# One step list per engine, one weight chunk and one token tile per step, in a two-block transformer on one core

## The reference

```python
h = rms_norm(x, g1); proj = h @ w_in                       # 5128 columns
qa,ka,va,qb,kb,vb,f,gate = split(proj)                      # 8 + 8 heads of 64
o_a = causal softmax attention(rope(norm(qa)), rope(norm(ka)), va)
o_b = the same with norm(qb), norm(kb), vb and a decay from cumsum(log_sigmoid(f))
merged = sigmoid(gate0)*(o_a @ w_branch_moba) + sigmoid(gate1)*(o_b @ w_branch_fox)
x = x + merged @ w_out
u,g = split(rms_norm(x, g2) @ w_ffn_up); x = x + (silu(conv3(g))*u) @ w_ffn_down
# second block
hq,hf,hi,hg,sq,sk,sv,iq,ik,iw,mq = split(rms_norm(x, g3) @ w_in_2)   # 3656 columns
mixed = concat(hgrn(hq,hf,hi,hg), attention over the best 64 keys by an index score(sq..iw),
               attention over mem with rms_norm(mem) @ w_mem_kv)
x = x + mixed @ w_out_2
a,b = split(rms_norm(x, g4) @ w_ffn_in_2); x = x + (silu(a)*b) @ w_ffn_out_2
```

## Time and profile before

| | us |
|---|---|
| median of 3 runs | 795.67 (795.42 to 797.9) |
| the profiled execution | 799.01 |
| its span, first to last instruction | 796.9 |
| mean granted TensorE clock | 0.970 of full speed |
| PE busy | 752.3 (94%) |
| DVE busy | 525.8 (66%) |
| ACT busy | 472.6 (59%) |
| chain that ended last: PE, DVE, ACT | 78%, 11%, 7% |
| weights and inputs read | 127 MB, 161 GB/s over the span |

### The profile page before, as it was taken

The page is one execution under the profiler, slowest core; times in us unless marked ns, Lnnn a source line. Parts: engine busy times, 40 slices in busy tenths (PEclk is TensorE's granted clock), DMA queues, the critical chain, the costliest instruction groups (busy, mean ns, idle before and its releaser), DMA issues.

```text
span 796.9 us, 10804 instructions
## 1 busy us (share of the span) xinstructions
PE 752.3 (94%) x3887; PEld 623.8 (78%) x3887; DVE 525.8 (66%) x811; ACT 472.6 (59%) x746; POOL 11.9 (1%) x18
## 2 busy tenths in 40 slices
PE   7999989999979999999999889897689999999998
PEld 4887879987778888888888777675568888888886
DVE  3777776686566878767365457998845666766540
ACT  3765667784256788776163695655724765676430
POOL 0014000000000000000000000000000000000000
PEclk7999999999989999999999999998899999999999
DMA  8657464444156664454475435331033666655640
GB/s 276 238 162 242 151 183 148 150 158 158 53 185 212 211 210 160 157 185 159 158 234 162 139 110 178 106 107 66 15 107 106 215 207 211 211 183 183 224 123 26
DMA packets 70985, 128.86 MB, mean 162 GB/s; under 512 B 5575, under 2 KB 17823, under 8 KB 70944
## 3 DMA queue, kind: packets, MB, share of 16 engines
q1 hardware_dynamic: 70366, 125.91, 48.6%
q10 hardware_dynamic: 578, 2.40, 0.9%
HBM read 127.24 MB, written 1.05 MB: 161 GB/s over the span
## 4 chain that ended last, share of the span: by engine, by line
PE 78%; DVE 11%; ACT 7%; issue 2%; DMA 1%; POOL 0%; ACTq 0%; DVEq 0%; POOLq 0%
PE acc L541 24%; PE acc L543 23%; PE acc L542 23%; DVE b_wlo L1466 3%; PE banks L692 1%; DMA b_raw<-in_w_in 1%; PE banks L604 1%; PE banks L558 1%; ACT b_whi L1007 1%; PE banks L633 1%; DVE b_ss L1537 1%; PE banks L735 1%; DVE b_qd L1917 1%; PE banks L885 1%; PE banks L619 0%
## 5 line engine op out<-in xcount | busy, mean ns | idle before, releaser
L1466 DVE TENSOR_TENSOR b_wlo<-b_raw,b_whi 128x1024 fp32r<-128x1024 f32 (+4 forms) x244 | 273.0, 1158 | 101.3 <-ACT b_whi L1007 100.1
L1007 ACT ACTIVATE b_whi<-b_raw 128x1024 fp32r<-128x1024 f32 (+4 forms) x244 | 235.8, 1002 | 88.7 <-PE acc L543 31.2
L541 PE MATMUL acc<-b_whi,b_hhi 128*128 128x512 f32 (+4 forms) x528 | 202.1, 383 | 5.5 <-DVE b_wlo L1466 2.2
L542 PE MATMUL acc<-b_whi,b_hlo 128*128 128x512 f32 (+4 forms) x528 | 197.3, 374 | 0.0
L543 PE MATMUL acc<-b_wlo,b_hhi 128*128 128x512 f32 (+4 forms) x528 | 196.9, 373 | 0.0
L541 PEld LDWEIGHTS acc<-b_whi,b_hhi 128*128 128x128 f32 x528 | 100.3, 190 | 24.7 <-issue 4.7
L541 PE MATMUL acc<-b_whi,b_ohi 128*128 128x512 f32 (+1 forms) x272 | 108.9, 400 | 9.9 <-DVE b_olo L1500 4.8
L543 PEld LDWEIGHTS acc<-b_wlo,b_hhi 128*128 128x128 f32 x528 | 100.1, 190 | 15.7
L542 PEld LDWEIGHTS acc<-b_whi,b_hlo 128*128 128x128 f32 x528 | 100.5, 190 | 14.6
L542 PE MATMUL acc<-b_whi,b_olo 128*128 128x512 f32 (+1 forms) x272 | 106.1, 390 | 0.0
L543 PE MATMUL acc<-b_wlo,b_ohi 128*128 128x512 f32 (+1 forms) x272 | 106.1, 390 | 0.0
(11 more groups left out here) (258 smaller groups left out, 755.5 us busy)
## 6 DMA issues: line engine op xcount, KB each, us to landing
b_raw<-in_w_in SPq DMA_DIRECT2D x48, 512.0 KB, 4.7
b_raw<-in_w_ffn_up SPq DMA_DIRECT2D x40, 512.0 KB, 4.8
b_raw<-in_w_ffn_in SPq DMA_DIRECT2D x40, 512.0 KB, 4.6
b_raw<-in_w_ffn_down SPq DMA_DIRECT2D x22, 512.0 KB, 5.6
b_raw<-in_w_ffn_out SPq DMA_DIRECT2D x22, 512.0 KB, 4.4
b_raw<-in_w_out SPq DMA_DIRECT2D x16, 512.0 KB, 4.2
b_raw<-in_w_in SPq DMA_DIRECT2D x12, 412.0 KB, 4.0
b_raw<-in_w_in SPq DMA_DIRECT2D x8, 410.0 KB, 3.9
```

The lines of the kernel that those rows point to most:

```text
L541: nc.tensor.matmul(o, a, wh, start=first, stop=False)
L542: nc.tensor.matmul(o, b, wh, start=False, stop=False)
L1007: A(whi[:, n % SPLIT, 0:c["nk"], 0:c["n"]], raw[:, n % RAW, 0:c["nk"], 0:c["n"]], ACT.Copy)\
L1466: V.tensor_tensor(wlo[:, n % SPLIT, 0:c["nk"], 0:c["n"]], raw[:, n % RAW, 0:c["nk"], 0:c["n"]], whi[:, n % SPLIT, 0:c["nk"], 0:c["n"]].bit ...
```

## The change

It does the same arithmetic with the same instructions, but for the order. The lists now run from the first norm to the last step before each feed-forward loop, on all three engines, and replace the hand-written pieces. A step ("gemm", name, c, t) is chunk c with token tile t; without t it is both. ("hi", name, c) and ("lo", name, c) say up to which chunk high and low parts are formed. Norms, sums leaving `acc`, the merge and head norms are steps by tile ("norm turn", "norm hi", "norm lo", "norm sum", "norm gain", "squares", "heads", "guess", "log", "split", "gate"). Weights are streamed in the order in which TensorE ends with them (its t = 1 steps). The last group of all, `d2_1`, does its last five chunks first with tile 0, then with tile 1. Ring sizes, buffers and banks stay. The lists have 178, 130 and 138 steps in ORDER1 (PE, ACT, DVE) and 167, 115 and 120 in ORDER2; here with the parts that are spoken of:

```diff
+ORDER1["pe"] = [("norm turn", "mem", 0, 0, 1), ("norm turn", "mem", 1, 0), ("gemm", "mkv", 0, 0), ("norm turn", "mem", 1, 1),
+     ("gemm", "mkv", 1, 0), ("gemm", "mkv", 0, 1), ("gemm", "mkv", 1, 1), ("norm turn", "x1", 0, 0),
...
+     ("gemm", "wo1_1", 1, 1), ("norm turn", "ffn1", 0, 0), ("gemm", "wo1_0", 2, 1),
+     ("gemm", "wo1_0", 3, 1), ("gemm", "wo1_1", 2, 1), ("gemm", "wo1_1", 3, 1), ("gemm", "u1s", 0, 0),
+     ("norm turn", "ffn1", 0, 1), ("gemm", "g1s", 0, 0), ("norm turn", "ffn1", 1, 0, 1), ("gemm", "g1s", 1, 0),
+     ("gemm", "g1s", 0, 1), ("gemm", "g1s", 1, 1), ("gemm", "u1s", 0, 1), ("gemm", "u1s", 1), ("gemm", "u1s", 2),
...
+ORDER1["dve"] = [("norm gain", "mem", 1, 0), ("norm gain", "mem", 0, 0), ("norm gain", "mem", 0, 1), ("lo", "mkv", 0),
+     ("norm lo", "mem", 0, 0), ("norm gain", "mem", 1, 1), ("lo", "mkv", 1), ("norm lo", "mem", 0, 1),
...
+ORDER2["pe"] = [("gemm", "d1_1", 0, 0), ("gemm", "d1_1", 1, 0), ("gemm", "d1_1", 0, 1), ("gemm", "d1_1", 2, 0),
+     ("gemm", "d1_1", 3, 0), ("gemm", "d1_1", 1, 1), ("gemm", "d1_1", 4, 0), ("gemm", "d1_1", 5, 0),
+     ("gemm", "d1_1", 6, 0), ("norm turn", "x2", 0, 0), ("gemm", "d1_1", 7, 0), ("gemm", "d1_1", 8, 0),
+     ("gemm", "d1_1", 2, 1), ("gemm", "d1_1", 3, 1), ("gemm", "d1_1", 4, 1), ("gemm", "d1_1", 9, 0),
...
+     ("gemm", "hq", 3, 1), ("gemm", "iqb", 1, 0), ("gemm", "hi", 0, 0), ("gemm", "iqb", 0, 1), ("gemm", "iqb", 1, 1),
+     ("gemm", "hi", 0, 1), ("gemm", "iqb", 2, 0), ("decay", 0), ("turn", "hk"), ("gemm", "iqb", 3, 0),
...
+     ("gemm", "hg", 3, 1), ("scores", 10), ("scores", 11), ("pairs", 7), ("gemm", "wo2_0", 3), ("hout", 3),
+     ("gemm", "wo2_1", 3, 0), ("probs", 10), ("pv", 10), ("gemm", "wo2_1", 3, 1), ("probs", 11), ("out", 0),
+     ("out", 2), ("pv", 11), ("gemm", "wo2_1", 0), ("gemm", "wo2_0", 0, 0), ("gemm", "wo2_0", 2, 0),
...
+ORDER2["dve"] = [("lo", "d1_1", 3), ("norm sum", "x2", 0, 0), ("norm gain", "x2", 0, 0), ("lo", "d1_1", 5),
...
+     ("log", "hf"), ("split", 0), ("log", "hq"), ("lo", "iqb", 3), ("gate", "q"), ("lo", "hi", 3), ("decay", 0),
+     ("lo", "sviq", 1), ("clear", 0), ("lo", "sviq", 3), ("pairs", 0), ("decay", 1), ("lo", "mq", 1), ("pairs", 1),
...
+     ("scores", 9), ("hout", 2), ("squares", "sqk"), ("pairs", 6), ("divide", 9), ("heads", "sqk"),
+     ("lo", "wo2_0", 3), ("pv", 9), ("best", 7), ("decay", 7), ("chosen", 0), ("scores", 10), ("lo", "wo2_1", 3),
+     ("log", "hg"), ("scores", 11), ("pairs", 7), ("gate", "g"), ("hout", 3), ("divide", 10), ("hgrn norm", 0),
+     ("divide", 11), ("hgrn norm", 1), ("pv", 10), ("hgrn norm", 2), ("lo", "wo2_1", 0), ("out", 0),
...
+    def listed(order):
+        for kind, n, *rest in order["pe"]:
+            if kind == "gemm" and rest[1:] != [0]:
+                lay(n, rest[0])
...
+            def chunk(name, c, t, i=0):
...
+                if t == 0:
                     pe.wait_ge(sem("lo ready"), n + 1 + PER * i)
+                if n == g["first"] and turn > 0:
+                    pe.wait_ge(sem(f"acc{p}{t} free"), turn + i)
+                if name in NORMED:
+                    pe.wait_ge(*at(f"bank{2 * t + c // PART} free", f"{NORMED[name]}T"))
...
-                gemm("d2_1")
+                gemm("d2_1", 0)
+                gemm("d2_1", 1)
+                gemm("d2_1", 2)
+                for t in range(T):
+                    for c in range(3 * PART, -(-FT // CK)):
+                        chunk("d2_1", c, t)
...
-                if kind == "gemm":
-                    hi_to(part_end(n, *rest) + 3 * PART)
+                if kind == "hi":
+                    hi_to(groups[n]["at"][rest[0]])
...
-                if kind == "gemm":
-                    lo_to(part_end(n, *rest) + 3 * PART)
+                if kind == "lo":
+                    lo_to(groups[n]["at"][rest[0]])
```

More of the change, by code:

```diff
@@ L156, in ffn @@
             add(f"d{m}_{c}", down, CN * c, CN, FT, "act")
[L158 to L164, removed]
-            stream(n, part=1)
-    for c in range(2):
-        add(f"wo2_{c}", "w_out_2", CN * c, CN, KT, "o")
-    stream("wo2_0", "wo2_1", part=1, order=[6, 0, 2, 4])
-    ffn(2, "w_ffn_in_2", "w_ffn_out_2", 0, DFF)
+    listed(ORDER1)
+    whole(*(f"{which}1_{j}" for j in range(PAIRS) for which in "gu"), "d1_0")
+    listed(ORDER2)
+    whole(*(f"{which}2_{j}" for j in range(PAIRS) for which in "gu"), "d2_0", "d2_1")
     return groups, chunks
@@ L552, in norm_T, with gemm @@
+                if t == T - 1:
+                    mm.then_inc(sem("chunk used"), 1)
+                elif n == g["last"]:
+                    mm.then_inc(sem("tile 0 summed"), 1)
+            def gemm(name, c=None, i=0):
+                lastc = len(groups[name]["at"]) - 1
+                for c in range(lastc + 1) if c is None else range(PART * c, min(PART * (c + 1), lastc + 1)):
+                    for t in range(T):
+                        chunk(name, c, t, i)
             def norm_T(k, b, tiles=range(T)):
@@ L696, in ffn1 @@
             def ffn1():
-                after_norm("ffn1", "g1s", "u1s")
                 ffn_T(1, "g", short="s")
@@ L1302, in _ @@
                 elif kind == "sums" and n in ("va", "vb"):
-                    for t in range(T):
+                    for t in rest:
                         a = sums(act, n, t)
                         leave(scaled(va[n == "vb"][:, t, :], a[:, :], ACT.Copy, "x1", t), n, t)
-                elif kind == "sums" and n[:2] == "fg":
+                elif kind == "gate log":
                     g = int(n[2:])
@@ L1531, in head_norm, with norm_step @@
-            def head_norm(step, src, sqs, heads, gains, width=DH, rope=False, name=None):
+                a = sums(dve, name, t)
+                cols = x[:, t, c * CN:(c + 1) * CN]
+                leave(V.tensor_tensor(cols, a[:, :], cols, ALU.add), name, t)
+            def norm_step(kind, k, *rest):
+                if kind == "norm sum":
+                    residual(f"{SUMMED[k]}{rest[0]}", rest[1])
+                elif kind == "norm gain" and k == "mem":
+                    c, t = rest
+                    norm_gain(k, memx, None, c, t, [(sem("mem gain spread"), 1), (sem(f"mem {t} in"), 16)])
+                elif kind == "norm gain" and k == "x1":
+                    c, t = rest
+                    norm_gain(k, x, gain, c, t, [gain_at(1), (sem(f"x {t} in"), 16), at(f"bank{2 * t + c} full", "memT")])
+                elif kind == "norm gain":
+                    c, t = rest
+                    norm_gain(k, x, gain, c, t, [gain_at({"ffn1": 2, "x2": 3, "ffn2": 4}[k]), moved(f"{SUMMED[k]}{c}", t)])
+                elif kind == "norm lo":
+                    norm_lo(k, *SIDE[k], rest[0], rest[1:])
+                elif kind == "norm root":
+                    norm_root(k)
```

662 lines of the change are left out of this document (287 added, 375 removed), and 53 rows, old and new, of the table pick.

## The result

The changed kernel takes 757.46 us in the median of 4 runs (756.83 to 758.33), the kernel before 796.78 in the same session (795.42 to 800.7). The ratio is 0.9507 with a 95% interval of 0.9474 to 0.9539, so 39 us or 4.9% less. Forecast were 765.4 and a range of 751 to 784: direction and range were right, the gain was three tenths larger than forecast (39.3 against 30.3), at the very edge of the forecast's own range of 757 to 775.

What follows compares the result with a forecast made beforehand. TensorE's idle time and the low clock behind it were taken as the bound, at most 51.0 us behind the front. Terms 2 + 3 + 7 + 17 + 0 + 1 + 0.3 = 30.3 gave 765.4 us, range 751 to 784.

Steps and rivals of the forecast that it cites:

- estimate of 752.5: Whole span by the skill's rule: 623.8 us of weight loads at the unbroken stretch's 0.829, a ceiling of 44 us gain.
- Front: Launch start: fewer steps ahead of the first product, at about 11.0, and perhaps earlier full clock; 2 us, bounds 0 and 4.7.
- Attention: Attention stage: chunk steps between dependent head steps close idle time and low clock; 3 us, bounds 0 and 5.
- Merge: Merge, w_out and ffn1 norm: the 4.2 us wait goes, on thin cover; 7 us, bounds 4 and 9.
- Middle: Middle stage: interleaved steps close TensorE's idle time and low clock, limited by VectorE's work; 17 us, bounds 10 and 26.4.
- `ffn2` norm: Norm before feed-forward two: tile 0's turn stands among wo2 products, but the sum is late; 1 us, bounds 0 and 3.5.
- the walk: Middle: VectorE's new list followed against ScalarE's and TensorE's with trace durations; VectorE still waits 9.5 us, length 122.9.
- The tail's low bound: Last 40 us of the middle: a long VectorE chain could keep all 10.6 us of TensorE's idle time, leaving a gain of 10.
- Tail: End of the launch: only the second sum's wait for the first and the joint write are saved; 0.3 us, 0 to 0.6.
- R1: Whole kernel: all gaps close, the middle reaching VectorE's 26.4 us; 42 to 43 us gain, 753 us; chance 0.15.
- R2: Whole kernel: gains given back as new waits replace old ones; about 12 us gain, 783 us; chance 0.15.
- R4: Weight ring: half-used chunks hold slots, high and low parts start late, kernel slower, 803 us at 0.33 a chunk; chance 0.07.

Runs made afterwards that it cites:

- e8_best_before: Kernel before, without rounds 4 to 7 of the search for the best keys (32 keys in place of 64): 798.70 us, ratio to before 1.0008.
- e2_joint_attn: Changed kernel, with every attention chunk (ka to fg4) used with both tiles at the place of its tile 1 step: 768.19 us.
- e6_squares: Changed kernel, with ScalarE forming both tiles' squares ahead of three of four high parts in the norm before feed-forward one, as before: 756.06 us.
- e7_best_after: Changed kernel, without rounds 4 to 7 of the search for the best keys (32 keys in place of 64): 755.47 us.
- e4_tail_order: Changed kernel, with the last 45 us of the middle back in the old order on all three engines: 764.53 us.
- e11_end: Changed kernel, with the last product d2_1 in parts with both tiles to the end, as before: 757.26 us.
- e10_better: Changed kernel, with the last norm's gains transferred early and the middle's tail reordered (on VectorE chosen, a low part and scores 10 ahead of decay 7): 755.47 us.
- e9_stalls: Changed kernel, with three stops of TensorE, made by GpSimd fills, put into stretches that have no gap: 769.76 us.
- e5_front: Changed kernel, with the first steps of all three lists at the very start in the order of before: 760.02 us.

## Why the prediction was right, and where not

**What bounds the kernel.** Right: TensorE's idle time and the clock behind it were all there was. 26.5 + 14.9 us came back of the 51 behind the front and what the front held, and the weight loads' share rose from 78 to 81%, against the 0.83 of the unbroken stretch. The Trainium skill, "Perfetto Trace Analysis", section "Identifying the Most-Contended Engine", says to judge the distance by the arithmetic done against the peak and by that share. The estimate of 752.5 that I made by it lies only 3 us under the span after (755.5), but that nearness is luck. It took the 623.8 us of weight loads as fixed, and they fell to 612.0 as the clock came back; 612.0/0.829 is 738. By that the kernel after has 17 us left, as many as its idle time of 18.1 says, so neither measure was the better one here.

**Front, 2 taken, 5.5 measured.** The first product was forecast at 11.0 and came at 10.67. The term was mis-sized, and the result lies above its bound of 4.7. I added the first product's 1.3 and a return of the clock, and nothing for the steps behind the first product. e8_best_before shows that the old front takes 31.6 even where the full clock is back before 20. At one pace and one kind of start the order is worth 3.9, of which 1.9 lie in those later steps; the other 1.6 are the launches' starts.

**Attention, 3 taken, 5.4 measured,** above the bound of 5.0. I held the 15 us of a head chain against 15 to 18 of products for thin and took off 2 for it. TensorE's waits in the stage after are 1.7 in all, none in a head chain. Part of the 5.4 is the low clock behind the wait of 2.14, which e8_best_before has without it (179.5, so 3.8). e2_joint_attn shows that the new order needs its tile steps as cover.

**Merge, 7 and 6.6.** Right, with a doubt that e6_squares took away.

**Middle, 17 taken, 22.7 measured.** This is the largest error of the sum. The step that failed is "VectorE alone has 113.4 of work, so no more than 26.4 can go", with 9.5 us that it would still idle. VectorE's work in the new middle was 105.1 and not 113.4, since low parts of weights, 7.3 us of them, moved out of it, most of them behind it (VectorE rose from 14.9 to 20.9 busy in the stage of the `ffn2` norm). A stage's work is no bound when the change moves the stage's edges. VectorE idled 15.8 us, not 9.5; but the stage as cut here begins 3.7 us earlier than the 139.8 of the forecast, and VectorE was idle for all of these 3.7 before, so the walk itself was short by 2.6. Too much work by 8.4 and too little idle by 2.6 make 5.8, the 5.7 that the term lacked but for rounding. The tail's low bound (all of 10.6 us idle stays) was carried by the belief that its chain is VectorE's work. e8_best_before and e7_best_after show that it isn't: 5.6 us of that work are worth 0.1 us of the middle in the old order and 0.3 in the new. The order of the same steps is worth 8.9 (e4_tail_order).

**`ffn2` norm, 1 and 1.4,** near by luck. There was 3.5 to have. The trace of after is the only one with a low clock there; eight others have the stage at 28.3 to 29.2, a gain of about 3. And the late transfer of the gains cost 1.4 to 3.6, since the stage takes 26.9 without it. My own account of what each moved step issues had not gone as far as `("gain", 0)`.

**Tail 0.3, loops 0.** −0.4 and 0.2. e11_end can't tell the end from nothing.

**The rivals.** R1 (753: all gaps close) was nearer than I gave it credit for: with the transfer repaired the kernel is at 754.6. Of the signs, the waits of 6.1 and 4.2 are gone and the middle's 120.9, in a cut 3.7 us wider, is somewhat below the 123 that I named, but VectorE's share in it is 87% and not 92%. R2's new waits exist (the gains, the waits of e10_better) but are small. R4, the ring, is out: one wait of 1.1 us for a low part, and no gain from using chunks at once. `d1_1` 8 to 10, the thinnest place, has no wait.

## What to carry to other kernels

When TensorE is nearly full, look for what stands ahead of the awaited instruction on the other engine's list before counting that engine's work: two steps there held the maximum back by 3 to 4 us, as the traces read, and leaving out 5.6 us of other work ahead of it brought nothing. Compare stages at the same product in both traces and not only medians: that showed 0.3 where the medians showed 2.0. Reckon with a low clock behind each wait of two microseconds or more, some 1.6 us more here where TensorE has full work behind it, but as a chance and not as a certainty up to 2.7. And go through a new list for its transfers by themselves, as one issued behind a step that waits is late by that wait.

## What the runs showed of the hardware

A stop of TensorE of 1.22 us left its clock alone, one of 2.39 and one of 4.13 were both followed by a single stretch of 3.4 us at about half speed; the 4.2 of before lies in one of 6.8. In all traces together low clock stood behind each of the nine stops of 3.4 us or more. Of those from 1.8 to 2.7 some had it behind them (1.84 in after, 2.12 and 2.14 in before, 2.16 to 2.18 in eight traces) and some had not (1.91 in e9_stalls, 2.11 in e5_front, 2.52 in e2_joint_attn). The same stop can do either. Before and e8_best_before have the same code at this place and the same stop; the row of before has the clock at 0.51, that of e8_best_before at 1.00, and the next matmul comes after 0.41 and 0.31 us (a timeline and a window row of each):

```profile
513.21 0.61 PE L872 MATMUL banks<-b_hgr,b_lfhi 128*128 128x512 f32 x1 [2.67 <-ACT b_spare L1417]
513.30:516.70 3.40, 3.40 (x10) 2.43 (x11) 3.21 (x7) 2.24 (x4) 0.00 (x0) 0.51 0.08 27
```
```profile
513.41 0.47 PE L872 MATMUL banks<-b_hgr,b_lfhi 128*128 128x512 f32 x1 [2.67 <-ACT b_spare L1417]
513.40:516.80 3.40, 2.73 (x13) 2.08 (x14) 3.19 (x8) 2.17 (x4) 0.00 (x0) 1.00 0.07 28
```

The start varies by 2 us: with the same code the first product came at 10.7 to 12.9. In the six late starts the profile's clock column shows 1.00 throughout, but four opening matmuls took 3.78 us instead of 2.0, and in e5_front and e8_best_before the first six product matmuls came 0.43 apart, the pace of 0.50. So the column can miss a stretch of low clock at the start; the spacing of equal matmuls shows it.

GpSimd multiplied 128x1024 in 2.35 us, where 8 times its 0.46 for 128 columns would be 3.7. While it did, four operations of VectorE took 2.22 us in place of 1.01.
